# Three of the eight feature chunks of a depthwise convolution computed on TensorE, as products with diagonal matrices

## What is computed

```python
CONV_WIDTH = 31
def conformer_conv(h, w1, b1, dw_w, dw_b, ln_g, ln_b, w2, b2):
    u = h @ w1 + b1                       # 1024 -> 2048
    a, g = jnp.split(u, 2, axis=-1)
    u = a * jax.nn.sigmoid(g)             # gated, 1024 features
    u = lax.conv_general_dilated(         # depthwise: each feature has 31 taps of its own, causal
        u, dw_w[:, None, :], window_strides=(1,), padding=[(CONV_WIDTH - 1, 0)],
        dimension_numbers=('NWC', 'WIO', 'NWC'), feature_group_count=D_MODEL) + dw_b
    u = jax.nn.silu(layernorm(u, ln_g, ln_b))
    return u @ w2 + b2
# after it: a mixture of experts (peer), attention, a second peer, and a second block
```

## Time and profile before

| what | value |
|---|---|
| time, three runs | 3219.94 us median (3217.9 to 3234.21) |
| the profiled execution's own time | 3240.0 us, its span 3238.2 us |
| PE, PEld busy | 91%, 87% of the span |
| DVE, ACT, POOL busy | 64%, 47%, 18% of the span |
| mean granted PE clock | 0.915 of full speed |

### The profile page before, as it was taken

The page is one execution under the profiler, slowest core; times in us unless marked ns, Lnnn a source line. Parts: engine busy times, 40 slices in busy tenths (PEclk is TensorE's granted clock), DMA queues, the critical chain, the costliest instruction groups (busy, mean ns, idle before and its releaser), DMA issues.

```text
span 3238.2 us, 61086 instructions
## 1 busy us (share of the span) xinstructions
PE 2957.0 (91%) x21442; PEld 2805.0 (87%) x21442; DVE 2076.8 (64%) x4503; ACT 1524.8 (47%) x3227; POOL 584.5 (18%) x646
## 2 busy tenths in 40 slices
PE   7189889999999989979889999999988889999998
PEld 7178779999999977678779999999987689986898
DVE  7947987777677654247887666666663656645565
ACT  5343244555555533233344555555542455554554
POOL 4621571000000011011670000000040320021100
PEclk9589899999999987579999999999985889988899
DMA  4025316677676532025316655555532025541364
GB/s 131 32 87 166 114 48 205 210 228 228 211 229 202 181 112 85 1 81 172 117 37 213 191 184 184 182 183 185 182 126 84 1 81 186 183 123 52 119 185 138
DMA packets 140745, 458.11 MB, mean 141 GB/s; under 512 B 15776, under 2 KB 33568, under 8 KB 140592
## 3 DMA queue, kind: packets, MB, share of 16 engines
q1 hardware_dynamic: 135120, 436.75, 42.7%
q0 software_dynamic: 5472, 19.41, 2.1%
HBM read 446.59 MB, written 9.50 MB: 141 GB/s over the span
## 4 chain that ended last, share of the span: by engine, by line
PE 49%; DVE 5%; ACT 1%; POOL 1%; issue 1%; DMA 0%; POOLq 0%; DVEq 0%; ACTq 0%; SPq 0%
PE banks L789 38%; PE banks L937 2%; PE banks L1122 1%; PE banks L914 1%; PE banks L1152 1%; PE banks L810 1%; POOL x_lo L2304 1%; PE banks L1036 1%; PE banks L1132 1%; DVE arena L1864 0%; DVE arena L1877 0%; PE banks L1114 0%; PE banks L1118 0%; DVE arena L1830 0%; DVE arena L1823 0%
## 5 line engine op out<-in xcount | busy, mean ns | idle before, releaser
L500 DVE TENSOR_TENSOR w_lo<-ring,w_hi 128x512 fp32r<-128x512 f32 x1464 | 1025.5, 706 | 756.9 <-ACT w_hi L493 750.5
L493 ACT ACTIVATE w_hi<-ring 128x512 fp32r<-128x512 f32 x1464 | 918.0, 631 | 957.3 <-PE banks L789 910.6
L789 PE MATMUL banks<-x_hi,w_hi 128*128 128x256 f32 (+2 forms) x3136 | 912.6, 291 | 54.7 <-POOL x_lo L2304 22.0
L789 PE MATMUL banks<-x_lo,w_hi 128*128 128x256 f32 (+2 forms) x3136 | 905.1, 289 | 0.0
L789 PE MATMUL banks<-x_hi,w_lo 128*128 128x256 f32 (+2 forms) x3136 | 903.0, 288 | 0.0
L789 PE MATMUL banks<-gated_hi,w_hi 128*128 128x256 f32 x2560 | 728.0, 284 | 10.2 <-DVE gated_lo L1957 10.0
L789 PE MATMUL banks<-gated_hi,w_lo 128*128 128x256 f32 x2560 | 727.2, 284 | 0.0
L789 PE MATMUL banks<-gated_lo,w_hi 128*128 128x256 f32 x2560 | 726.0, 284 | 0.0
L789 PEld LDWEIGHTS banks<-x_hi,w_hi 128*128 128x128 f32 x3136 | 613.2, 196 | 65.6 <-issue 44.1
L789 PEld LDWEIGHTS banks<-x_hi,w_lo 128*128 128x128 f32 x3136 | 613.6, 196 | 0.0
L789 PEld LDWEIGHTS banks<-x_lo,w_hi 128*128 128x128 f32 x3136 | 613.1, 195 | 0.6
(11 more groups left out here) (308 smaller groups left out, 2978.3 us busy)
## 6 DMA issues: line engine op xcount, KB each, us to landing
ring<-in_peer_v SPq DMA_DIRECT2D x256, 512.0 KB, 3.5
ring<-in_peer_u SPq DMA_DIRECT2D x192, 512.0 KB, 3.6
arena<-in_peer_u SPq DMA_DIRECT2D x64, 512.0 KB, 3.6
ring<-in_mlp_up SPq DMA_DIRECT2D x64, 512.0 KB, 3.5
ring<-in_mlp_down SPq DMA_DIRECT2D x64, 512.0 KB, 3.5
ring<-w_peer_query SPq DMA_DIRECT2D x32, 512.0 KB, 3.5
ring<-w_fox_proj SPq DMA_DIRECT2D x24, 512.0 KB, 3.5
ring<-w_nsa_proj SPq DMA_DIRECT2D x20, 512.0 KB, 3.5
```

The lines of the kernel that those rows point to most:

```text
L493: act.activation(w_hi[:, hn % SPLITS], raw_half(hn), ACT.Copy).then_inc(hi_ready, 1)
L500: dve.tensor_tensor(w_lo[:, hn % SPLITS], raw_half(hn), w_hi[:, hn % SPLITS].bitcast(F32), ALU.subtract)\
L789: mm = pe.matmul(out, w_at(w), x, start=start and j == 0, stop=stop and j == 2, skip_group_check=True)
```

## The change

PE takes feature chunks 5, 6 and 7. DVE keeps 0, 2 and 4, POOL (with ACT) keeps 1 and 3. For each of PE's 93 taps ACT makes a 128x128 diagonal matrix, the identity scaled for each partition with the tap (`spread_taps`), 5 behind each of the 16 chunks of `conv_in` and 13 in `conv_taps`. In `conv_taps` PE multiplies each with the shifted `glu_u`, in plain fp32, and accumulates the 31 products of a feature chunk in one PSUM bank; ACT then adds the bias and writes `conv_y`. The taps beside `conv_in` become 2 for DVE and 3 for POOL.

```diff
+        diagonals = cv(3 * CONV_W, P)
...
-        POOL_CONV = (1, 3, 5)
+        POOL_CONV, PE_CONV = (1, 3), (5, 6, 7)
...
-        DVE_TAPS = [(c, w) for c in range(NC) if c not in POOL_CONV for w in range(CONV_W)]
+        DVE_TAPS = [(c, w) for c in range(NC) if c not in POOL_CONV + PE_CONV for w in range(CONV_W)]
         POOL_TAPS = [(c, w) for c in POOL_CONV for w in range(CONV_W)]
-        DVE_BESIDE, POOL_BESIDE = 5, 4
+        PE_TAPS = [(c, w) for c in PE_CONV for w in range(CONV_W)]
+        DVE_BESIDE, POOL_BESIDE, PE_BESIDE = 2, 3, 5
...
+            def conv_taps(s):
+                pe.wait_ge(glu_done, NC)
+                for n, (c, w) in enumerate(PE_TAPS):
+                    pe.wait_ge(diagonal_ready, n + 1)
+                    mm = pe.matmul(banks[:, 4 + n // CONV_W, 0:T0], diagonals[:, n], glu_u[:, c, w:w + T0], start=w == 0,
+                                   stop=w == CONV_W - 1)
+                    if w == CONV_W - 1:
+                        mm.then_inc(conv_summed, 1)
...
                         weigh_taps(pool_taps_beside(m))
+                        spread_taps(PE_BESIDE * m, PE_BESIDE * (m + 1))
...
+            def spread_taps(first, last):
+
+                for n, (c, w) in list(enumerate(PE_TAPS))[first:last]:
+                    act.activation(diagonals[:, n], ident, ACT.Copy, scale=taps[:, w * NC + c:w * NC + c + 1])\
+                       .then_inc(diagonal_ready, 1)
+
             def conv_taps_(s):
+                spread_taps(PE_BESIDE * 16, len(PE_TAPS))
                 weigh_taps(POOL_TAPS[POOL_BESIDE * 12:])
+                for i, c in enumerate(PE_CONV):
+                    act.wait_ge(conv_summed, i + 1)
+                    act.activation(conv_y[:, c], banks[:, 4 + i, 0:T0], ACT.Identity, bias=vec("a_dw_b", 0, c))
```

More of the change, by code:

```diff
@@ L260, in build_program @@
         taps = cv(CONV_W * NC)
+        diagonals = cv(3 * CONV_W, P)
+        assert cv.at <= ARENA - (NC * T0 + 3 * T0)
         pv = Carve()
@@ L403, in build_program @@
         taps_landed = sem("taps_landed")
+        diagonal_ready, conv_summed = sem("diagonal_ready"), sem("conv_summed")
         subkeys_landed = sem("subkeys_landed")
@@ L1253, in _ @@
                          nsa_proj=nsa_proj, nsa_compress=nsa_compress, turn_out=turn_out, fox_proj=fox_proj,
-                         subln=lambda s: None, conv_taps=lambda s: None, norm_add=lambda s: None)[kind](s)
+                         subln=lambda s: None, conv_taps=conv_taps, norm_add=lambda s: None)[kind](s)
                 end_stage(pe, s)
```

## The result

The changed kernel takes 3190.52 us (median of 10 runs, 3186.56 to 3204.88), the kernel before 3220.14 us (10 runs, 3216.75 to 3239.04): a ratio of 0.9909, with a 95% interval of 0.9886 to 0.9931. The medians lie 29.6 us apart; 33 were forecast. The profiled execution took 3192.16 us. The times of one kernel lie in two groups (before: eight runs of 3217 to 3224 and two of 3234 and 3239; after: seven of 3187 to 3192 and three of 3204 to 3205), so that a median depends on how many runs fell into each; the medians of the lower groups alone lie 31.0 us apart.

What follows compares the result with a forecast made beforehand. DVE's taps were taken to bound conv_taps and DVE to bound conv_in. Layer norm start -30.9 us and its matmuls -2.5 gave -33.4, from the median 3219.94 to 3187 (3175 to 3208; main case, chance 0.72, 3175 to 3196).

Steps and rivals of the forecast that it cites:

- What bounds the kernel: In conv_taps DVE's taps set the end at 162.0 us, and everything behind is a chain through PE that shifts with it.
- The rival of no effect: In conv_taps: the change does nothing because something other than DVE's taps sets the end; chance 0.03.
- The rival of dear diagonals: In conv_in: ACT's diagonals cost as 272 columns, conv_taps starts at 95, time 3196; no chance of its own given.
- The clock in `conv_in`: Rival: PE's clock swings at short pauses, six of twelve chunks low, conv_taps 12.6 us later, 3200; 0.15 including other give-backs.
- The products: In conv_taps: PE's 93 products take 0.456 us each, 42.4 us in all, with their waits hidden.
- The rival with unhidden weights: In conv_taps: weight loads don't run under the products, 1.16 us a product, 108 us for 93, time 3250; chance 0.04.
- the low clock throughout: Rival in conv_taps: all 93 products run at the low clock, 84.8 us, layer norm at 171.4, time 3229; chance 0.06.
- The clock spell: At the start of conv_taps: PE idles 8 us, then a spell at the low clock costs 2.2 us.
- DVE beside PE: In conv_taps: DVE's remaining work takes 41.4 us and ends at 127.4, with PE last by 3 us.
- Behind the products: In the layer norm: its eight matmuls run at the high clock, 3.65 us instead of 6.11, saving 2.5.
- the small matmuls, squares and roots: 0: Behind the layer norm's eight matmuls: these idle and restart as before, so they change by 0 us.
- its 20 us from the profiled time to the median: Whole kernel before: the profiled execution, 3240.0 us, lies 20 us above the median of 3219.94.

Runs made afterwards that it cites:

- Experiment 3: Kernel before with all eight feature chunks of taps on DVE and none on POOL (GpSimd): 3233.14 us (10 runs) against 3223.28, ratio 1.000.
- experiment 6: Changed kernel with feature chunk 5 given back to DVE, so PE keeps only 6 and 7: 3201.18 us (one run).
- Experiment 4: Changed kernel with three diagonals instead of five behind each weight chunk, the other 45 made after conv_in: 3186.67 us (one run).
- experiment 1: Changed kernel without the barrier behind conv_in, each product waiting only for its own feature chunk: 3190.04 us (one run).
- experiment 2: Changed kernel with no taps on POOL: DVE takes feature chunks 0 to 4, ACT weighs none: 3181.91 us (4 runs), ratio to before 0.986.
- experiment 8: Changed kernel with ACT's order in conv_taps reversed, weighed taps for POOL ahead of the last 13 diagonals: 3190.11 us (one run).
- experiment 7: Kernel before, its division of taps kept, with ACT also making the 93 diagonals that nobody reads: 3246.32 us (one run).
- experiment 5: Changed kernel with no taps on POOL (DVE chunks 0 to 4) and no barrier behind conv_in: 3180.68 us (6 runs), ratio to before 0.9844.
- experiment 9: Changed kernel without POOL taps or the barrier behind conv_in, plus nine unread products on PE behind the 93: 3199.8 us.

## Why the prediction was right, step by step

- **What bounds the kernel.** DVE's taps set the end of `conv_taps` and everything behind shifted with them: taking them away moved the layer norm's first matmul by 30.5 us (30.9 forecast). Experiments 3 and 6 move it by taps of DVE alone. The rival of no effect is out.
- **`conv_in`.** Forecast 3.95 us for a chunk, bounded by ACT, and its end at 86; measured 3.93 and 85.9. The diagonal had been set at 0.29 us from a slope, between 0.10 and 0.413: it is 0.29 from start to start and 0.393 long. Experiment 4 confirms the bound by moving it: the start of `conv_taps` came 5.1 us earlier. The rival of dear diagonals is out.
- **The clock in `conv_in`.** The rival wanted swings between the two levels. In each window of 4 us from 44 to 76 PE was busy 3.15 to 3.52 us, and the granted clock was 1.00. The Trainium skill's rule on short pauses (TensorE: Matmul & The Clock Gate, "A second HAM failure mode: psum-queue depth-cycling") did not show in these pauses.
- **The products.** Forecast 0.456 us each from two records of 0.228; experiment 1 has 0.460 at the full clock. The weight loads ran under them (186 loads of 0.189 us, median, beside 186 products that follow one another without a gap), and so did the waits. The rival with unhidden weights, 1.16 us each, is out, and so is the low clock throughout: 0.95 was granted in the stage.
- **The clock spell.** Forecast 2.2 us after 8 idle ones; the idle time was 8.05, and experiment 1 against the changed kernel gives 45.00 - 42.81 = 2.2. That it is just this number is partly luck: the same 93 products took 44.81 (experiment 4), 45.70 (2) and 45.85 us (8) behind 6.05, 5.23 and 8.04 idle ones, 2.0 to 3.0 more than 42.81.
- **DVE beside PE.** Forecast 127.4, measured 127.5, though POOL went another way than the sum supposed: 34 us and not 24.7. The end of DVE doesn't depend on when POOL works, only on how many taps it has: from the first tap left over to the last addition DVE took 41.45 to 41.48 us in the changed kernel and in experiments 1, 4 and 8, with POOL starting 0.5, 3.8, 4.3 or 13.7 us after it.
- **Behind the products.** The layer norm's eight matmuls took 3.94 us instead of 6.11: -2.2, with -2.5 forecast. DVE's copy behind them came 32.7 us earlier than in the profile of before (135.57 against 168.28).
- **The term that was mis-sized** is "the small matmuls, squares and roots: 0". The clock fell sooner behind the now quick layer norm, and the 42 small matmuls, 6.49 us in the profile before, took 7.66: +1.2. The projection behind them lost another 0.8. So -30.7 us was left at the start of the experts (243.1 against 273.8) where -33.4 had been forecast. The rows of before, from the timelines of DVE and PE:

```profile
168.28 0.44 DVE L1797 COPY arena<-banks 128x272 f32<-128x272 f32 x1 [6.31 <-PE banks L864]
```

```profile
171.61 6.49 PE L810 MATMUL banks<-const_a,arena 128*128 128x1 f32 x42 [1.10 <-ACT arena L1263]
```

- **The profiled executions** lie 47.8 us apart (3240.0 and 3192.16), and not 33. The shift is 32.1 us when the products of the first attention (L1199, after the change L1212) begin (1276.7 against 1244.6) and 52.2 when they end (1386.5 against 1334.3): 20.1 us arise there, where that execution of the kernel before stayed at the low clock longer (last section). In the second attention 4.5 us of them are lost again. This belongs to the execution and not to the change, which the sum had allowed for with its 20 us from the profiled time to the median. The 30.7 us account for all of the medians' 29.6, within what the runs can tell.

## What to carry to other kernels

Where two engines share a slowdown, price the second engine's work in what it costs the first: a GpSimd tap cost DVE some 0.5 us, and DVE does that tap itself in 0.415. A diagonal product in fp32 (0.46 us for 272 columns, with 0.29 us of ScalarE for the diagonal) pays for a depthwise tap only while PE would otherwise be idle and DVE ends last; what it saves is read from the engine that ends last, here 3.4 us short of the next one. And count the idle time of PE ahead of and behind each edit: the same eight matmuls took 3.94 or 6.65 us by what PE did before, which ate more than half of what experiment 1 had won.

## What the runs showed of the hardware

**GpSimd beside VectorE.** A DVE tap takes 0.415 us alone and 0.82 to 0.875 beside POOL, POOL's addition 0.92 to 0.96. In experiment 8, 29 taps of DVE took 23.73 us, of which POOL worked beside them up to 110.9, 21.0 us. That is time for 23 of its taps (0.913 each; the last is the addition of the two sums), and they cost DVE 23.73 - 12.05 = 11.7 us, 0.51 each. Experiment 3 gives the same: DVE did 93 taps (38.6 us) and three additions (1.3) more and ended 6.2 us sooner, so POOL's 93 taps had cost it 46.1 us, 0.50 each. That is more than their help is worth. The Trainium skill (SBUF — State Buffer, "SBUF: two separate sides") says that a VectorE operation with two SBUF inputs and a GpSimd operation that reads SBUF exclude each other for a whole instruction; alternation of the two, as in experiment 8, fits it. That a single addition was shut out for 10.65 us, while some 25 instructions of DVE passed, is more than one instruction's turn. It came in the changed kernel and, with 5.86 us, in experiment 7. In both the held addition came to its end 0.6 us after DVE's run of like taps had ended (101.01 after 100.40, 115.51 after 114.89), and in experiment 4 a first addition of 1.31 us did so too (95.95 after 95.34). But in experiment 1 POOL also began in the middle of such a run and alternated at once, so what brings it on is open.

**The clock in the attention.** At the same work of the first block's attention the kernel before (1320 us on) and the changed kernel (1288 us on) both begin at the low clock with PE busy all the time; then the one stays there and the other doesn't. Windows of 20 us of before, then of after:

```profile
1320.00:1340.00 20.00, 20.00 (x60) 13.44 (x60) 4.78 (x15) 3.55 (x12) 0.00 (x0) 0.50 0.00 1
1340.00:1360.00 20.00, 20.00 (x65) 14.13 (x62) 3.99 (x13) 5.33 (x18) 0.00 (x0) 0.50 0.00 0
```

```profile
1288.00:1308.00 20.00, 20.00 (x61) 13.50 (x61) 4.78 (x15) 3.55 (x12) 0.00 (x0) 0.50 0.00 0
1308.00:1328.00 20.00, 20.00 (x111) 14.45 (x110) 7.73 (x25) 7.31 (x25) 0.00 (x0) 0.98 0.01 1
```

Ahead of the convolution's products a PE fully busy by its records had its clock back some 4 us after the first of them (6 in experiment 8). Here the low clock stayed for some 75 us in the changed kernel and for some 140 in the kernel before. In both pairs of profiles that differ so (before and after, experiments 5 and 9) the stretch of work is 20.1 us longer with the long spell. Of the eleven profiled executions three have the long spell: that of the kernel before (3240.0 us), of experiment 7 (3246.32) and of experiment 9 (3199.8). The other eight stay low for 65 to 75 us, among them that of the changed kernel (3192.16) and those of experiments 2, 3 and 5, none of which lies near the top of its kernel's times. So the difference has the size and the place to be what spreads the times of one kernel over some 20 us. That it is so is argued and not shown, since only profiled executions show their clock, and what decides between the two spells is open.
